# Sliding-window attention inside a projection: group copies moved ahead of the weight split, attention steps moved ahead of rotations

## The reference, cut to what matters

```python
def swa_mixer(h, positions, w_in, sinks, w_out):      # 16 query heads, 4 key/value heads, head width 64
    q, k, v, z = jnp.split(h @ w_in, ...)             # 1024, 256, 256, 1024 columns
    q = rope(q, positions); k = rope(k, positions)
    # blocks of 128 queries see their own and the previous 128 keys, masked to a window of 128
    s = einsum(q, k) / sqrt(64); logits = where(mask, s, -inf)
    m = maximum(max(logits), sink); e = exp(logits - m)
    p = e / (sum(e) + exp(sink - m))
    return (einsum(p, v) * silu(z)) @ w_out
```

## Time and profile before

| | |
|---|---|
| median of 3 executions | 2250.15 us (2249.4 to 2252.83) |
| the profiled execution | 2247.12 us, its span 2245.4 us |
| PE busy | 2167.7 us (97% of the span) |
| DVE busy | 1141.6 us (51%) |
| ACT busy | 866.2 us (39%) |
| POOL busy | 413.1 us (18%) |

### The profile page before, as it was taken

The page is one execution under the profiler, slowest core; times in us unless marked ns, Lnnn a source line. Parts: engine busy times, 40 slices in busy tenths (PEclk is TensorE's granted clock), DMA queues, the critical chain, the costliest instruction groups (busy, mean ns, idle before and its releaser), DMA issues. The chain is left out here.

```text
span 2245.4 us, 29101 instructions
## 1 busy us (share of the span) xinstructions
PE 2167.7 (97%) x10810; PEld 1750.9 (78%) x10810; DVE 1141.6 (51%) x1823; ACT 866.2 (39%) x1422; POOL 413.1 (18%) x454
## 2 busy tenths in 40 slices
PE   7999999999999999999899999999999998999999
PEld 6888887766677888888788878886788887886667
DVE  5444323644466444323575544335566686665444
ACT  4322223564334222223432233225446753543453
POOL 2111101212324111000220010001110242024441
PEclk9999999999999999999999999999999997999999
DMA  4333333611112333333233346750143211243111
GB/s 143 112 94 95 101 94 83 112 47 57 57 47 76 110 95 93 106 94 88 66 106 95 94 72 104 93 97 11 48 127 90 67 50 36 67 109 66 48 47 47
DMA packets 359450, 182.13 MB, mean 81 GB/s; under 512 B 42053, under 2 KB 356142, under 8 KB 358958
## 3 DMA queue, kind: packets, MB, share of 16 engines
q1 hardware_dynamic: 359000, 180.57, 32.2%
q10 hardware_dynamic: 342, 0.12, 0.0%
HBM read 176.14 MB, written 4.52 MB: 80 GB/s over the span
## 5 line engine op out<-in xcount | busy, mean ns | idle before, releaser
L329 PE MATMUL ps<-xh,wh 128*128 128x512 f32 x1904 | 757.7, 398 | 1.5 <-DVE wl L296 1.5
L331 PE MATMUL ps<-xh,wl 128*128 128x512 f32 x1904 | 742.4, 390 | 0.0
L330 PE MATMUL ps<-xl,wh 128*128 128x512 f32 x1904 | 741.5, 389 | 0.0
L296 DVE TENSOR_TENSOR wl<-raw,wh 128x1024 fp32r<-128x1024 f32 x328 | 416.4, 1270 | 400.7 <-ACT wh L286 395.6
L286 ACT ACTIVATE wh<-raw 128x1024 fp32r<-128x1024 f32 x328 | 341.3, 1043 | 359.9 <-PE ps L331 313.2
L329 PEld LDWEIGHTS ps<-xh,wh 128*128 128x128 f32 x1904 | 357.5, 188 | 83.7 <-issue 10.6
L331 PEld LDWEIGHTS ps<-xh,wl 128*128 128x128 f32 x1904 | 357.4, 188 | 76.3
L330 PEld LDWEIGHTS ps<-xl,wh 128*128 128x128 f32 x1904 | 357.8, 188 | 72.4 <-issue 2.4
L471 POOL TENSOR_TENSOR acc<-acc,sq 128x512 f32<-128x512 f32 x72 | 101.6, 1412 | 258.8 <-ACT sq L913 166.2
L478 PE MATMUL ps<-xh,wh 128*128 128x512 f32 x288 | 121.1, 421 | 20.9 <-ACT xh L410 8.1
L329 PE MATMUL ps<-a_hi,wh 128*128 128x512 f32 x352 | 137.0, 389 | 0.0
(11 more groups left out here) (414 smaller groups left out, 2547.7 us busy)
## 6 DMA issues: line engine op xcount, KB each, us to landing
raw<-in_w_ffn_gate SPq DMA_DIRECT2D x44, 512.0 KB, 3.8
raw<-in_w_ffn_up SPq DMA_DIRECT2D x44, 512.0 KB, 3.8
raw<-in_w_ffn_down SPq DMA_DIRECT2D x32, 512.0 KB, 3.9
raw<-in_conv_w_in SPq DMA_DIRECT2D x32, 512.0 KB, 4.0
raw<-in_fox_w_in SPq DMA_DIRECT2D x32, 512.0 KB, 11.5
raw<-in_gdn_w_in SPq DMA_DIRECT2D x32, 512.0 KB, 4.1
raw<-in_w_in SPq DMA_DIRECT2D x24, 512.0 KB, 3.8
raw<-in_swa_w_in SPq DMA_DIRECT2D x32, 256.0 KB, 3.8
```

Source lines behind the costliest of these rows:

```text
L296: nc.vector.tensor_tensor(wl[s][:, 0:kb, :], raw[r][:, 0:kb, :], wh[s][:, 0:kb, :].bitcast(F32), ALU.subtract).then_inc(lo_done, 1)
L329: pe.matmul(o, wh[s][:, kb, :], x_hi, start=start, stop=False)
L330: pe.matmul(o, wh[s][:, kb, :], x_lo, start=False, stop=False)
L331: return pe.matmul(o, wl[s][:, kb, :], x_hi, start=False, stop=stop)
```

## The change

Three things are done, all in the stage `swa_in`. The group copies of steps 11, 15, 23 and 27 leave the DVE part of their step (`ahead`), and are done by `between` at the start of the tile whose first step they belong to (tiles 11, 13, 16 and 18), before the tile's weight split. In tiles 7 to 12 DVE and POOL do the attention steps of a tile first and its rotation after them (`steps_first`). The order on PE and ACT stays as it was.

```diff
-        def pair_steps(name, pairs, groups, Z, PT, ctx, banks, pack=False, sink=None, last=0):
+        def pair_steps(name, pairs, groups, Z, PT, ctx, banks, pack=False, sink=None, last=0, ahead=()):
...
+            def take(dve, s):
+                g = last_of[s - 4]
+                dve.wait_ge(pv_done, B + 2 * (s - 4) + 2)
+                nc.vector.tensor_copy(groups[g][1], ps[PV][:, :]).then_inc(o_taken, 1)
+
             def dve_step(dve, s):
-                if s - 4 in last_of:
-                    g = last_of[s - 4]
-                    dve.wait_ge(pv_done, B + 2 * (s - 4) + 2)
-                    nc.vector.tensor_copy(groups[g][1], ps[PV][:, :]).then_inc(o_taken, 1)
+                if s - 4 in last_of and s not in ahead:
+                    take(dve, s)
...
+                def steps_first(k):
+
+                    todo = items(k)
+                    return [w for w in todo if w[0] == "c"] + [w for w in todo if w[0] != "c"] if 6 < k < 13 else todo
+
+                def between(dve, i, j, part):
+                    for kind, x in items(4 * i + j) if part == 1 else ():
+                        if kind == "c" and x in (11, 15, 23, 27):
+                            at_take(dve, x)
...
                     for k in range(20):
-                        for kind, x in items(k):
+                        for kind, x in steps_first(k):
                             pool_do(pool, kind, x)
...
-                    for kind, x in items(k):
+                    for kind, x in steps_first(k):
                         dve_do(dve, kind, x)
```

More of the change, by code:

```diff
@@ L1402, in act_step @@
                         nc.scalar.activation(PT[:, 0, h, 0:d["klen"]], ps[TR[h]][:, 0:d["klen"]], ACT.Copy).then_inc(pt_done, 1)
-            return pe_step, dve_step, pool_step, act_step
+            return pe_step, dve_step, pool_step, act_step, take
         with ExitStack() as c:
@@ L1581, in kernel_program @@
             n["lots"] += G8
-            ch_pe, ch_dve, ch_pool, ch_act = pair_steps("ch", pairs, groups, ch_room[:, 0:4, :].rearrange("p (r h) q -> p r h q", r=2),
+            ch_pe, ch_dve, ch_pool, ch_act, _ = pair_steps("ch", pairs, groups, ch_room[:, 0:4, :].rearrange("p (r h) q -> p r h q", r=2),
                                                           ch_room[:, 4:6, :].rearrange("p (r h) q -> p r h q", r=1), c, ((2, 3), (4, 5), OUT), last=3)
@@ L3105, in kernel_program @@
                 g_swa = n["groups"]
-                at_pe, at_dve, at_pool, at_act = pair_steps("swa", pairs, groups, zr, zt, c2, ((2, 3), (4, 5), PV), True,
-                                                            (lambda u: heads(0, u), lambda u: heads(1, u)), last=2)
+                at_pe, at_dve, at_pool, at_act, at_take = pair_steps("swa", pairs, groups, zr, zt, c2, ((2, 3), (4, 5), PV), True,
+                                                            (lambda u: heads(0, u), lambda u: heads(1, u)), last=2, ahead=(11, 15, 23, 27))
                 AU = len(pairs)
@@ L3290, in kernel_program @@
                 rr, rr_n = dve_link, steps_
-                in_proj("swa_in", vA[:, col["norm_w_2"] + 3 * DB:col["norm_w_2"] + 4 * DB], None, sums=sums, block=block, pro=pro, evac_dve=swa_evac,
+                in_proj("swa_in", vA[:, col["norm_w_2"] + 3 * DB:col["norm_w_2"] + 4 * DB], None, sums=sums, block=block, pro=pro, evac_dve=swa_evac, between_dve=between,
                         tails=dict(sp=sp_tail, pool=pool_tail, pe=pe_tail, dve=dve_tail, act=act_tail),
```

## The result

The changed kernel takes 2265.84 us (median of 6 executions, 2264.53 to 2274.55), the kernel before 2249.78 (6 executions, 2246.45 to 2252.83): a ratio of 1.008, 95% interval 1.0064 to 1.0095. It is slower, by 16.1 us in the medians, where 19.3 were forecast. The profiled execution of after took 2267.55 us, span 2265.8, so 20.4 us more than the span of before.

A forecast was written before the change was run, and what follows sets the result against it. PE, busy for nearly the whole span, was taken as the bound. Net 12.4 us lost in waits plus 6.9 us of clock falls make 19.3 us, so 2250.15 becomes 2269.5 us, range 2260 to 2278.

The forecast's parts named there:

- The chain: Tiles 8 to 12: scaling, rotation, sum and evacuation in series make PE's rotations come later, by 13.18 us in all.
- The wins: PE waits shortened or gone: 1.04 us in tile 7, 1.4 at c9, 0.86 at c11, 0.8 for c23 and c27.
- c9's and c11's waits: Tiles 10 and 11: the scaling wait at c9 and the copy wait before c11 go, giving back 1.4 and 0.86 us.
- Tile 13: No rotation there, but tile 12's late evacuation delays c15's maximum and scaling, so PE transposes 2.3 us later.
- c23 and c27: Copies moved ahead of the split at these steps: 0.2 and 0.6 us won, 0.8 together.
- the give-back that I reasoned with: At moved copies, the step's maximum and POOL's scaling move up only about 0.6 us, so PE waits for the scaling next.
- The clock: PE's clock falls in three of the five new waits, 2.3 us each: 6.9 us, bounds none and 15.3.
- That the clock stays up: Rival: the chain's loss of 12.4 us in full, without clock falls: 2262.6 us; chance 0.20.
- Five long falls: Rival: the clock falls for long in all five new waits, 15.3 us: 2277.9 us; chance 0.17.
- A hidden evacuation: Rival: the late evacuation costs PE nothing, only wins of 4.7 us stand: 2245.4 us; chance 0.05.
- the rotation behind the tile's last step on both engines: Tiles 7 to 12: the rotation stands behind the last step on DVE and POOL, the evacuation behind it; 6.76 us chain.

The follow-up runs named there:

- e1_copies: Changed kernel with steps and rotations back in the old order, only the four group copies moved: ratio 0.9993 to the kernel before, 2244.32 us.
- e4b_pe_busy: Changed kernel with 10, 7, 14, 11 and 9 useless matmuls filling PE's waits before the rotations of tiles 8 to 12: ratio 1.0055 to before, 2260.59 us.
- e5_pool_back: Changed kernel with POOL's old order put back (rotation first, then steps), DVE's order as changed: ratio 0.9986 to the kernel before, 2244.36 us.
- e3_evac_first: Changed kernel with DVE's rotation of tiles 7 to 12 moved behind the tile's evacuation, POOL's order as changed: ratio 0.9999 to before, 2246.94 us.
- e2_steps: Changed kernel with the group copies back in their old places, steps still ahead of rotations in tiles 7 to 12: ratio 1.0085 to before, 2266.87 us.
- e6_split_late: From e5_pool_back, DVE also does steps c15, c20 and c27 ahead of the weight split: ratio 0.9982 to the kernel before, 2242.78 us.

## Why the prediction was right, and where its sizes were off

**The chain** held as worked out. From c3's scores to the next rotation it took 6.69 us (2047.85 to 2054.54; forecast 6.76), from c5's 6.08 (6.12), from c12's 6.22 (6.29). The five waits were 2.62, 1.93, 3.44, 2.76 and 2.29, together 13.0; forecast were 2.7, 2.3, 3.7, 3.0 and 2.5, so 14.2. The largest error is tile 9's 0.4: I gave it tile 12's distance of 3.78 us, since the layout is the same, and never read its own row (3.99, 2059.42 to 2063.41 in PE's timeline of before), which accounts for half of it. POOL's product took 1.26 to 1.29 us in all six tiles, as assumed: it met no split.

**The wins** held too. c9's and c11's waits went (1.4 and 0.86), and c3's went altogether (1.25; I had it shrink by 1.04). Tile 13 lost 2.12 (1.16 + 0.45 before, 2.15 + 1.58 after; forecast 2.3). c23 and c27 won 1.04 (0.47 + 1.84 of copy waits gone, c28's scaling wait up from 0.44 to 1.71; forecast 0.8). That is the give-back that I reasoned with, and e1_copies shows it alone. The sum of waits is 10.6, against 12.4.

**The clock** was mis-sized the other way: 9.8 us against 6.9. I counted falls by length, three of the five waits, at 2.3 each. There were four in the five, of 2.0 on average, and one behind c28's grown wait, which I had not foreseen. Counting by length was the wrong step: 1.93 and 1.71 us brought the clock down, and 2.62 in the same execution did not. The trace of the kernel before already spoke against it: I wrote that waits of 0.9 to 1.8 us left the clock at 1.00, but the wait of 1.49 us at 2182.99 has a fall behind it. The Trainium skill (TensorE: Matmul & The Clock Gate, HAM oscillation) tells of a kernel in which the clock comes down again behind a wait in every round, with waits of some 3 to 5 us. Of the waits here only tile 10's is as long, and the clock fell behind it; it fell behind shorter ones too, but not behind every one.

**Luck in the total.** The two errors nearly cancel in the profiled execution (20.4 against 19.3), and that is luck: the chain came out 1.8 us cheaper and the clock 2.9 us dearer. The median difference is smaller, 16.1. The profile of before lies 2.7 us under the median of before, and that of after 1.7 us over the median of after. As the falls differ between profiles of the same waits, their number in other executions is a likely reason, which no profile of those executions shows.

**The rivals.** That the clock stays up is out (the windows). e4b_pe_busy, with the clock up in tiles 8 to 12, is 12.8 us slower than before, where this rival named 12.4; but the falls left in its profile, in tile 13 and at c28, are part of that. Five long falls did not come. A hidden evacuation is out: PE stopped before L3145 in all five tiles.

**What I had not separated.** The prediction put the loss on "the rotation behind the tile's last step on both engines". The runs split that. With DVE's half alone (e5_pool_back) the kernel gains, so the loss needs POOL's half. It also needs DVE's sum ahead of the evacuation: with that sum behind the evacuation and POOL's order as changed (e3_evac_first) the loss is gone too. POOL's half alone was not run, and the order of the instructions forbids it: DVE's sum would wait for POOL's product, which stands behind a scaling that waits for a reciprocal, which stands behind that sum on DVE.

## What to carry to other kernels

When two engines' queues are reordered together, work out the chain for each reordering alone: here the move on DVE alone did no harm, and the move on POOL on top of it brought the loss, because POOL's share of the rotation had been hidden only while it stood first. Before moving work ahead of something, look at what stands behind it in the same queue and who waits for that; here it was an evacuation that PE needed. And a wait removed is not won until the next wait of the same step has been looked at: of 4.3 us of copy waits, 1.9 came back one step later.

## What the runs showed of the hardware beyond the forecast

- The length of a PE wait did not decide whether the clock fell. In the profile of after it held behind tile 8's 2.62 us and fell behind tile 9's 1.93; in that of e2_steps it fell behind 2.61 and held behind 1.91. Behind the wait of 1.72 us at c28 it fell in e1_copies (0.72 over 6 us) and held in e5_pool_back (1.00 from 2160 to 2175).
- POOL's scaling of two 128x256 tiles took 1.82 to 1.84 us without a DVE instruction of two SBUF inputs beside it, 2.05 with a rotation's sum beside it (such an instruction), and 2.75 to 2.76 with a weight split beside it (another), three times out of three in e6_split_late. The Trainium skill (SBUF — State Buffer, Who interferes with whom) says that a DVE instruction with two SBUF inputs and a GpSimd instruction that reads SBUF shut each other out for the whole of the one that came first. These rows agree in direction: the scaling lost 0.9 us beside a split of 1.23, and 0.2 beside a sum of 0.69, so less than the whole of either.
- One added float32 matmul of 128 columns took 0.24 us of PE at a granted clock of 1.00 (2.39 us for ten, which the trace shows as 20 rows).
